# Order of the overflow chunks in a mixture-of-experts stage: chunk number j at position 2j+1, in place of turns from the front and from the back

## The reference, cut to what matters

```python
def hier_moe(h, w_rg, b_rg, w_re, b_re, w1, w3, w2):
    x = h.reshape(b * s, d)
    _, g_idx = lax.top_k(g_logits, 1)            # 1 of 4 groups
    e_val, e_idx = lax.top_k(e_logits, TOP_K_FINE)   # 2 of its 4 experts
    e_gate = jax.nn.softmax(e_val, axis=-1) * g_gate
    combine = ...                                # (544, 16), two entries a row
    hid = jax.nn.silu(x @ w1[e]) * (x @ w3[e])   # w1, w3: 16 x 1024 x 256
    hid = hid * combine
    return einsum('nef,efd->nd', hid, w2)        # w2: 16 x 256 x 1024
```

## Time and profile before

| | |
|---|---|
| median of 3 runs | 1449.36 us (1448.5 to 1455.18) |
| the profiled execution's own time | 1449.5 us |
| its span | 1447.8 us |
| TensorE busy | 1191.5 us (82%) |
| VectorE, ScalarE, GpSimd busy | 444.4, 285.3, 228.2 us |
| moved by DMA | 306.55 MB, 212 GB/s over the span |
| TensorE's mean granted clock | 0.904 of full |

### The profile page before, as it was taken

One profiled execution on the slowest core, in us unless ns is written; L12 is line 12 of the kernel. 1 busy time (PEld: TensorE's weight loads), 2 busy tenths in 40 slices (PEclk: granted clock), 3 DMA queues, 4 the chain that ended last, 5 costly groups with the idle time before them and its releaser, 6 DMA issues.

```text
span 1447.8 us, 21265 instructions
## 1 busy us (share of the span) xinstructions
PE 1191.5 (82%) x7743; PEld 804.9 (56%) x7743; DVE 444.4 (31%) x1088; ACT 285.3 (20%) x613; POOL 228.2 (16%) x307
## 2 busy tenths in 40 slices
PE   4599999977899999967788888879997478878890
PEld 2377777555577777744555555547545344444440
DVE  4200000374322223224444344435355211111116
ACT  2200001142222222212222222222211011111112
POOL 1000000050011112200000000000000344444530
PEclk9899999998799999988989998879997588889995
DMA  8814432139435421089887998758504477888965
GB/s 306 308 43 169 140 116 106 31 117 318 174 119 205 147 76 45 1 285 306 285 281 254 296 302 292 272 198 326 169 33 171 164 302 303 314 315 332 402 253 195
DMA packets 112835, 306.55 MB, mean 212 GB/s; under 512 B 18966, under 2 KB 33071, under 8 KB 103472
## 3 DMA queue, kind: packets, MB, share of 16 engines
q1 hardware_dynamic: 95600, 251.93, 49.2%
q0 software_dynamic: 16576, 49.10, 9.2%
q10 hardware_dynamic: 576, 4.46, 0.8%
HBM read 304.35 MB, written 45.81 MB: 242 GB/s over the span
## 4 chain that ended last, share of the span: by engine, by line
PE 65%; SPq 9%; issue 9%; DVE 7%; DMA 6%; ACT 2%; another core or an unknown queue 1%; POOL 0%; DVEq 0%; POOLq 0%; ACTq 0%
PE psum L894 57%; PE psum L1195 4%; SPq L590 3%; SPq L594 3%; DMA wring<-in_w_mod 3%; DVE arena L1793 2%; PE psum L1459 1%; PE psum L1234 1%; SPq L532 1%; DMA hT<-gate_tiles 1%; PE psum L1116 1%; DVE wring L1801 1%; DMA xT<-in_cache_kv 1%; DVE arena L1801 1%
## 5 line engine op out<-in xcount | busy, mean ns | idle before, releaser
L894 PE MATMUL psum<-hT,wring 128*128 128x272 f32 x1216 | 291.9, 399 | 8.3 <-ACT hT L1515 8.3
L894 PEld LDWEIGHTS psum<-hT,wring 128*128 128x128 f32 x1216 | 231.5, 193 | 70.0 <-issue 22.2
L894 PE MATMUL psum<-arena 128*8 128x128 f32 (+5 forms) x1432 | 155.3, 329 | 6.4 <-DVE arena L1793 3.5
L894 PE MATMUL psum<-wring,arena 128*8 128x128 f32 (+4 forms) x1104 | 142.9, 435 | 15.5 <-DMA wring<-in_w_mod 9.9
L894 PEld LDWEIGHTS psum<-arena 128*8 128x8 f32 (+3 forms) x1432 | 83.8, 112 | 58.5 <-issue 42.7
L894 PE MATMUL psum<-arena,hT 128*64 128x256 f32 x640 | 85.2, 426 | 27.0 <-issue 26.8
L894 PEld LDWEIGHTS psum<-wring,arena 128*8 128x8 f32 (+3 forms) x1104 | 59.4, 114 | 79.3 <-issue 65.1
L807 POOL TENSOR_SCALAR wring<-wring,arena 128x384 f32<-128x384 f32 (+6 forms) x32 | 45.6, 1425 | 254.3 <-DVE arena L2050 254.3
L894 PEld LDWEIGHTS psum<-arena,hT 128*64 128x64 f32 x640 | 50.9, 154 | 55.1 <-issue 36.6
L894 PE MATMUL psum<-hT,arena 128*128 128x272 f32 (+1 forms) x280 | 70.2, 422 | 8.5 <-DMA arena<-in_w_in 8.5
L755 DVE COPY arena<-psum 128x512 f32<-128x512 f32 x64 | 44.2, 691 | 101.0 <-PE psum L894 51.7
(11 more groups left out here) (244 smaller groups left out, 1355.0 us busy)
## 6 DMA issues: line engine op xcount, KB each, us to landing
arena<-in_cache_kv SPq DMA_DIRECT2D x128, 320.0 KB, 3.5
wring<-in_w_mod SPq DMA_DIRECT2D x12, 2048.0 KB
xT<-in_cache_kv SPq DMA_DIRECT2D x64, 320.0 KB, 3.5
wring<-in_cache_kv SPq DMA_DIRECT2D x64, 320.0 KB, 3.5
arena<-in_w SPq DMA_DIRECT2D x20, 1024.0 KB
out_dil_sample<-in_cache_dil SPq DMA_DIRECT2D x8, 2044.0 KB, 10.8
wring<-in_w_in SPq DMA_DIRECT2D x6, 2048.0 KB
wring<-in_w SPq DMA_DIRECT2D x12, 1024.0 KB
```

Of the source, the lines that this page charges most:

```text
L894: return T.matmul(out, lhsT, rhs, start=start, stop=stop, **k)
```

## The change

The table is counted straight up, and the formula on VectorE becomes position = 2j+1, which needs one instruction where three stood.

```diff
@@ -435,7 +435,7 @@
         PV_STEPS = 6
         W_LOADS = (11, 11, 10)
-        OVER_AT = [n // 2 if n % 2 == 0 else OVER - 1 - n // 2 for n in range(OVER)]
+        OVER_AT = list(range(OVER))
         FIRST = (0, 1)
@@ -2377,9 +2377,7 @@
             link(tt(r_p1, r_p1, r_q, ALU.add))
-            link(ts(r_p2, r_p1, -4.0, 67.0, ALU.mult, ALU.add))
-            link(ts(r_p1, r_p1, 4.0, -3.0, ALU.mult, ALU.add))
-            link(tt(r_p1, r_p1, r_p2, ALU.min))
+            link(ts(r_p1, r_p1, 2.0, -1.0, ALU.mult, ALU.add))
             link(stt(r_ch, r_ch, 2.0, r_p1, ALU.mult, ALU.subtract))
```

## The result

The changed kernel takes 1430.47 us (median of 4 runs, 1429.35 to 1437.17) against 1451.34 us (median of 4, 1448.5 to 1455.18). The ratio is 0.9855, 95% interval 0.9818 to 0.9892: about 21 us or 1.5% faster, more than the 0.5% under which a difference can't be told from none. The forecast was 1433.8 us, with a range of 1427.5 to 1451.

The account below looks back on a forecast made before the run. TensorE was taken to be bound by waits for weights, with DMA left holes by the order of issue. Terms -19.9 - 0.4 + 0 + 2.1 + 2.5 = -15.7 us gave 1433.8 us, range 1427.5 to 1451.

Parts of the forecast that it names:

- waits and groups at the lower clock after chunk 19 gone: TensorE ahead of chunks 21, 25 and 27: waits of 14.9 us and slower groups of 5.0 us go, -19.9 us.
- chunk 0 to 5, with the load at 3: Chunk 3's new load moves while DMA is idle and costs nothing; upper bound 2 us.
- loads at 7, 11, 15, 19: New real loads: +0.7 us per cycle at 7, 11, 15, +2.1 in all; +2.5 at 19, not given back later.
- VectorE: Two of three linked instructions go, all on the path TensorE waits for: -0.4 us.
- tail: Read-back waits for the last scatter; chunk 31 now scatters no bytes: nothing, at best -1.7 us.
- The form of the waits: TensorE waits still ahead of 9, 13 and 17; short ones (1 to 3 us) at 7, 11, 15 and 19.
- the rival of no change: Pairs of chunks 5 to 19 move at 351 GB/s, 20.0 us each: +0.8 us net, 1450 us; chance 0.13.
- The slower rival: New loads at 7, 11, 15, 19 miss the holes, 7.6 us each: +9.9 us, 1459.4 us; chance 0.12.

Follow-up runs that it names:

- e2: The kernel before with every empty overflow chunk loading the last expert, so all 16 overflow loads are real: 1449.53 us, ratio to before 0.9998, stage 265.3 us.
- e6: The kernel before with the gathers of w1 and w3 of chunk c+5 issued ahead of the scatter of c: 1418.27 us, ratio to before 0.9752.
- e11: The changed kernel with real overflow chunks last (position 31-2j) and w1 and w3 gathered ahead of the scatter: 1425.27 us, ratio to before 0.9818.

## Why the prediction was right

Point by point, from the two profiled executions:

| step | forecast | measured |
|---|---|---|
| waits and groups at the lower clock after chunk 19 gone | -19.9 | -20.1 |
| chunk 0 to 5, with the load at 3 | 0 | -0.6 |
| loads at 7, 11, 15, 19 | +2.1 +2.5 | +3.8 |
| VectorE | -0.4 | -0.4 |
| tail | 0 (to -1.7) | -0.5 |
| sum | -15.7 | -17.8 |

*After 19.* From the start of chunk 19 to the last outputs it was 1410.68 - 1308.69 = 102.0 us, now 1391.08 - 1306.18 = 84.9: -17.1. In it chunk 19's own group is 3.0 us longer (6.65 against 3.67) because it now follows a wait; without that it is -20.1, the 19.9 of the forecast.

*Up to 19.* Chunk 5 to 19 went from 118.94 to 119.75 us, +0.8, and the 3.0 us at 19 belong to the same loads: +3.8 against 4.6. The sum was near, but only because its two parts were off in opposite directions, which was luck. From chunk 5 to 17 it was 104.66 us and is 102.65: the loads at 7, 11 and 15 cost -2.0, where I had +2.1. From 17 to 19 it was 14.28 us and is 17.10; with the group at 19 that is +5.8, where I had +2.5. The form of the waits was wrong: I had short waits of 1.4 us at 7, 11 and 15 and the long ones kept at 9, 13 and 17. They came out at about 3 us each. The size of the pair (17.1 us) follows from bytes and rate, where I took 16.75 from a single pair that had moved 6.97 MB. And the group at the lower clock behind the new wait at 19 was missing from my sum.

*VectorE.* In the timeline of VectorE after, one instruction stands where three stood, and the next one starts 0.21 us later, not 0.62:

```profile
1125.66 0.17 DVE L1798 TENSOR_SCALAR arena<-arena 128x10 f32<-128x10 f32 x1
1125.87 0.37 DVE L1801 SCALAR_TENSOR_TENSOR arena<-arena 128x10 f32<-128x10 f32 x2
```

This saving can't be seen apart from the 0.5 us between the first weight loads and chunk 0. The remaining 2.3 us between the profiled executions lie ahead of the stage, and no experiment speaks of them: that the measured time came out below the forecast is in part this scatter.

*The rate.* It decided between the forecast and the rival of no change, which took 351 GB/s. The dense stretch kept 417 GB/s for 120 us. The 358 GB/s per core of "DMA: Bandwidth & Descriptors" (Trainium skill, section Specifications) did not limit this run of one core alone. The mean of the dense stretch and each of its slices (at most 430 GB/s) stayed under the 435 GB/s that the same section of the Trainium skill gives as the ceiling of the fabric, though single slices of under 1 us read 439 to 466 GB/s in the earlier trace rows.

*The slower rival* said that the new loads would take time from others, 7.6 us each. e2 excludes it: six added loads and no longer stage.

*What I had not asked*: whether the order by turns was bad in itself. e6 shows that it is the better of the two orders once the gathers aren't late. The change went round the cause of the holes; it didn't remove it.

## What to carry to other kernels

Before a load is counted as the bound, look at the slices of DMA within one cycle: a cycle with holes can take one more transfer for nothing, and then the empty slots of a fixed schedule are wasted there. The better cure is to issue the next load on the condition that it really needs (the slot read) and ahead of work that waits for something later; after that, spread the loads so that DMA and the compute engine end together. And when the start of a stage scatters by more than 10 us, compare the stage, not the whole.

## What the runs showed of the hardware

After each wait of about 3 us the following matmul group ran partly at the lower level, 1.2 GHz: 5.0 to 5.3 us and not 3.67 behind waits of 2.9 to 3.4 us (granted clock 0.70 over the group of chunk 7), and 6.65 us behind the one at chunk 19 (3.29 us, 0.54). The length of the wait alone does not settle it: e2's group at chunk 29 took 5.36 us behind a wait of 1.41 us (0.68), and e11's at chunk 15 stayed at 3.67 us behind one of 2.22 us (1.00). So the eight waits after, 29.4 us together, still cost 13.2 us in slower groups behind them, where the seven before, 44.5 us together, cost 15.0.

Two queues, one fed by GpSimd's indirect gathers and one by SyncE, together kept 417 GB/s with no slice under 396 over 120 us, row gathers and scatters among them. GpSimd took 1.0 us for each indirect DMA it issued, with 0.3 us between two, whether it moved a megabyte or, with all its indices out of bounds, nothing: the first gather of chunk 7 (empty before) and that of chunk 9 (real) both read 1.04 us in the earlier trace rows.
